# A hybrid attention and convolution layer: another order for deferred VectorE work, gate units and the first merge steps

## The reference

```
h    = rms_norm(x)
proj = h @ w_in                       # q k v z_a | glu (2048) | z_c | gate_a gate_c
A:  q, k rotated in part; 8 heads, two softmax maps of 64 dims each, causal
    o = softmax(q1 k1) v - lam * softmax(q2 k2) v
    y_attn = (rms_norm(o) * silu(z_a)) @ w_o_attn
B:  u = glu(...); causal depthwise conv of 31; layer_norm; silu
    y_conv = (u * silu(z_c)) @ w_pw2 + b_pw2
m   = sigmoid(gate_a) * y_attn + sigmoid(gate_c) * y_conv
out = x + rms_norm(m @ w_out)
```

## Time and profile before

| | us |
|---|---|
| median of 3 runs (1183.11 to 1189.87) | 1183.71 |
| the profiled execution | 1181.25 |
| its span on the slowest core, core 6 | 1179.7 |
| spans of the even cores 0, 2, 4, 6 | 1177.5, 1176.5, 1179.7, 1179.7 |
| spans of the odd cores 1, 3, 5, 7 | 1169.8, 1171.2, 1171.2, 1168.9 |
| PE busy on core 6 | 1096.0 (93%) |
| DVE busy | 551.1 (47%) |
| ACT busy | 323.7 (27%) |

### The profile page before, as it was taken

How to read it: one execution, slowest core, us unless ns; L and a number is a source line. 1 busy time by engine, 2 the same in 40 slices (tenths; PEclk the granted TensorE clock), 3 DMA queues, 4 the chain that set the end, 5 groups by cost and what they waited for, 6 DMA issues and landing times.

```text
span 1179.7 us, 21808 instructions; the slowest of 8 cores (1168.9 to 1179.7 us)
## 1 busy us (share of the span) xinstructions
PE 1096.0 (93%) x8042; PEld 674.0 (57%) x8042; DVE 551.1 (47%) x1290; ACT 323.7 (27%) x500; POOL 102.1 (9%) x196
## 2 busy tenths in 40 slices
PE   2699999999999998899888999999999999999995
PEld 1355556886666774577444566666666666654442
DVE  5573444426556136766677633333333333315333
ACT  3442223432101165566444311111111111102111
POOL 1111010011101100000000001101101010000000
PEclk9899999999999998899899999999999999999998
DMA  8929767554665632322142305337266183064442
GB/s 251 220 46 174 143 114 150 106 86 81 139 135 113 139 57 57 57 49 51 37 73 37 55 18 108 55 53 114 46 128 110 34 144 57 16 179 161 158 160 95
DMA packets 49792, 118.11 MB, mean 100 GB/s; under 512 B 5520, under 2 KB 11920, under 8 KB 46352
## 3 DMA queue, kind: packets, MB, share of 16 engines
q0 software_dynamic: 27648, 62.93, 32.8%
q1 hardware_dynamic: 21744, 53.53, 14.9%
q10 hardware_dynamic: 288, 0.18, 0.0%
HBM read 162.94 MB, written 16.58 MB: 152 GB/s over the span
## 4 chain that ended last, share of the span: by engine, by line
PE 81%; DVE 9%; issue 3%; DMA 3%; ACT 3%; DVEq 0%; SPq 0%; ACTq 0%
PE ps L1291 21%; PE ps L816 11%; PE ps L1343 11%; PE ps L770 10%; PE ps L649 9%; PE ps L1301 5%; PE ps L1295 5%; PE ps L693 3%; PE ps L1021 2%; PE ps L922 2%; DMA r<-usc 2%; PE ps L899 2%; DVE zoz L970 1%; DVE r L1028 1%; DVE r L958 1%
## 5 line engine op out<-in xcount | busy, mean ns | idle before, releaser
L1291 PE MATMUL ps<-hTo,wring 128*128 128x384 bf16 x1536 | 257.5, 326 | 0.0
L1291 PEld LDWEIGHTS ps<-hTo,wring 128*128 128x128 bf16 x1536 | 150.3, 98 | 99.2
L164 POOL DMA_DIRECT2D wring<-wp x176 | 93.4, 549 | 835.9 <-PE ps L1291 242.0
L649 PE MATMUL ps<-hTo,wring 128*128 128x384 bf16 x768 | 130.9, 332 | 9.9 <-ACT hTo L545 4.2
L770 PE MATMUL ps<-wring,hTo 128*128 128x256 bf16 x1152 | 135.6, 273 | 1.2 <-PE ps L899 1.2
L1308 ACT ACTIVATE zoz<-zoz 128x384 f32<-128x384 f32 x96 | 50.0, 522 | 315.3 <-DVE zoz L1306 315.3
L816 PE MATMUL ps<-hTo,wring 128*128 128x384 bf16 x768 | 125.0, 326 | 0.0
L770 PEld LDWEIGHTS ps<-wring,hTo 128*128 128x128 bf16 x1152 | 108.6, 98 | 21.2 <-issue 8.3
L1306 DVE TENSOR_TENSOR zoz<-ps,R 128x384 f32<-128x384 f32 x96 | 53.5, 558 | 128.0 <-PE ps L1291 127.8
L649 PEld LDWEIGHTS ps<-hTo,wring 128*128 128x128 bf16 x768 | 75.6, 100 | 63.1 <-issue 16.5
L905 ACT ACTIVATE r<-ps 128x1024 bf16<-128x1024 f32 (+2 forms) x104 | 92.8, 905 | 47.6 <-PE ps L899 44.2
(11 more groups left out here) (114 smaller groups left out, 1016.1 us busy)
## 6 DMA issues: line engine op xcount, KB each, us to landing
wring<-wp POOLq DMA_DIRECT2D x176, 256.0 KB, 7.1
r<-usc SPq DMA_DIRECT2D x32, 295.2 KB, 8.2
hTo<-xr SPq DMA_DIRECT2D x9, 1024.0 KB, 6.8
out<-hTo SPq DMA_DIRECT2D x18, 512.0 KB, 3.3
r<-xf SPq DMA_DIRECT2D x11, 768.0 KB, 9.2
r<-wop POOLq DMA_DIRECT2D x4, 1024.0 KB, 13.8
zoz<-wop POOLq DMA_DIRECT2D x4, 1024.0 KB, 14.9
r<-wout POOLq DMA_DIRECT2D x4, 1024.0 KB, 20.5
```

The source lines that it names most:

```text
L164: eng.dma_start(out=it[1][0], in_=it[1][1]).then_inc(self.dsem[it[2]], 16)
L649: t.op('pe', lambda e, dc=dc, x=x: e.matmul(bank(2 * par + x, n), lhsT=w[:, dc, 128 * x:128 * x + 128], rhs=hTo[:, dc, c:c + n], start=(dc ...
L1291: t.op('pe', lambda e, dc=dc, k=k, w=w, o=o, cs=cs, c0=c0, n=n: e.matmul(o[k], lhsT=w[:, dc, cs], rhs=hTo[:, dc, HALO + c0:HALO + c0 + n], ...
```

## The change

- **Deferred operations.** `spent` keeps an estimate of the time that TensorE and VectorE have been given so far; QK, masks, PV, fill pieces, z operations and deferred operations each add a constant. `pump` issues a deferred operation only if its `ready` time has come and VectorE's estimate is at most 0.5 us ahead of TensorE's. It is called at each step and after each fill piece. `H.rate` is gone.
- **z units.** With the last piece only the read from PSUM is issued. Tanh and the two products go to a list `zlate`, of which each step issues one entry: tanh one step later, the products a step after that. A new unit issues what is left first.
- **Quarters.** Half 0 has column blocks 0, 1 | 2, 3 | 4 | 5, 6, 7 of z, half 1 has 0 | 1 | 2, 3 | 4 to 7. Two weight panels change places accordingly.
- **Merge.** The step is split into `merge_head` (gates, conv branch) and `merge_tail` (the rest). Two heads, of steps 0 and 1, are issued before `f_begin`, which transposes with banks 2 and 6 instead of 6, 7, 4 and 5.

```diff
+++ after.py
@@ -208,15 +208,15 @@
     p = [rng(C_GLU + 128 * c, 128) + rng(C_GLU + 1024 + 128 * c, 128) for c in range(8)]
     p += [rng(C_ZA + 256 * g) for g in range(4)]
     p += [dims(C_Q, j) for j in range(4)] + [dims(C_K, j) for j in range(4)]
-    p += [rng(C_V), rng(C_V + 256), rng(C_ZC), rng(C_V + 512), rng(C_V + 768), rng(C_ZC + 256), rng(C_ZC + 512), rng(C_ZC + 768)]
+    p += [rng(C_V), rng(C_V + 256), rng(C_ZC), rng(C_V + 512), rng(C_ZC + 256), rng(C_V + 768), rng(C_ZC + 512), rng(C_ZC + 768)]
     for k in range(8):
         p += [rng(C_GA + 256 * k), rng(C_GC + 256 * k)]
     return p
 
 
 P_GLU, P_ZA, P_Q0, P_Q, P_K0, P_K, P_F = 0, 8, 12, 13, 16, 17, 28
-P_V = (20, 21, 23, 24)
-P_ZC = (22, 25, 26, 27)
+P_V = (20, 21, 23, 25)
+P_ZC = (22, 24, 26, 27)
 LAST = {0: 2, 1: 2, 2: 3}
 ND = 144
 
@@ -232,14 +232,14 @@
             self.xtg = ()
             self.fg = ((0, 384), (384, 384), (768, 384))
             self.slots = ((0, 2), (2, 2), (4, 2), (6, 2), (8, 1))
-            self.rate = 6
+            self.fill = ((('v', 1), ('z', 0, 1)), (('v', 2), ('z', 2, 3)), (('v', 3), ('z', 4)), (('z', 5, 6, 7),))
         else:
             self.first, self.no, self.halo, self.nx = 1152, 896, 32, 1152
             self.xg = ((0, 288), (288, 320), (608, 320))
             self.xtg = tuple((160 * k, 160) for k in range(7))
             self.fg = ((0, 448), (448, 448))
             self.slots = ((0, 1), (1, 2), (3, 2), (5, 2))
-            self.rate = 4
+            self.fill = ((('v', 1), ('z', 0)), (('z', 1), ('v', 2)), (('z', 2, 3), ('v', 3)), (('z', 4, 5, 6, 7),))
         self.nh = self.no + self.halo
         self.nu = self.no + 32
         self.nt = self.no // 128
@@ -886,6 +886,11 @@
 
 
     pairs = [(h,) + st for h in range(8) for st in H.steps()]
+    now = {'pe': 0.0, 'dve': 0.0}
+
+    def spent(e, us):
+
+        now[e] = (max(now['dve'], now['pe']) if e == 'dve' else now['pe']) + us
     NS = len(H.slots)
 
     def emit_qk(n):
@@ -901,6 +906,7 @@
                     rhs=QT[hp][64 * c:64 * c + 64, 128 * q0 + qo:128 * q0 + qo + qn], start=True, stop=True),
                     reads=rd, writes=[('ps', pb + c)], sig=(k == len(ent) - 1 and c == 1))
         w = sum(x[2] for x in ent)
+        spent('pe', w / 1280.0)
         src = ps[:, 512 * pb:512 * pb + 1024].rearrange("p (c n) -> p c n", c=2)[:, :, 0:w]
         t.op('act', lambda e: e.activation(out=et[:, :, 0:w], in_=src, func=AF.Exp, scale=0.125),
              reads=[('ps', pb), ('ps', pb + 1)], writes=[('ET', n % 3)])
@@ -909,6 +915,7 @@
                 v = et[:, :, o:o + 128]
                 t.op('dve', lambda e, v=v: e.tensor_tensor(out=v, in0=v, in1=tri.unsqueeze(1).to_broadcast([128, 2, 128]), op=ALU.mult),
                      reads=['cb', ('ET', n % 3)], writes=[('ET', n % 3)])
+                spent('dve', 0.3)
 
     def emit_pv(n):
         h, si, q0, nq, ent, first, last = pairs[n]
@@ -924,15 +931,31 @@
                     start=(begin and c == 0), stop=(final and c == 1)),
                     reads=[('ET', n % 3), ('VA', slot, kt), ('Vone', slot)], writes=[('ps', 4 + sub)],
                     sig=c == 1 and (i == len(todo) - 1 or final))
+        spent('pe', 0.16 * len(todo))
         if last:
             finalize(h, si, q0, nq)
 
     late = []
+    zlate = []
     oz_done = set()
 
     def run_late(n):
         for _ in range(min(n, len(late))):
-            late.pop(0)[1]()
+            _, _, cost, f = late.pop(0)
+            spent('dve', cost)
+            f()
+
+    def pump():
+
+        while late and late[0][1] <= now['pe'] and now['dve'] <= now['pe'] + 0.5:
+            run_late(1)
+
+    def run_zlate(flush=False):
+
+        while zlate:
+            zlate.pop(0)()
+            if not flush:
+                return
 
     def finalize(h, si, q0, nq):
         fk = NS * h + si
@@ -946,6 +969,7 @@
             t.op('act', lambda e: e.activation(out=ac, in_=src, func=AF.Copy), reads=[('ps', 4 + b) for b in range(nq)], writes=[an])
         else:
             t.op('dve', lambda e: e.tensor_copy(out=ac, in_=src), reads=[('ps', 4 + b) for b in range(nq)], writes=[an])
+            spent('dve', 0.7)
         f = [lambda: t.op('dve', lambda e: e.reciprocal(out=rs, in_=ac[:, :, :, 128]), reads=[an, 'small'], writes=[('rs', fk)]),
              lambda: t.op('dve', lambda e: e.tensor_scalar(out=rs[:, :, 1], in0=rs[:, :, 1], scalar1=neglam, scalar2=None, op0=ALU.mult),
                           reads=[('rs', fk), 'neglam'], writes=[('rs', fk)]),
@@ -961,7 +985,8 @@
                   lambda sub=sub, oi=oi, on=on, i=i: t.op('dve', lambda e: e.scalar_tensor_tensor(
                       out=t0s[:, sub, :], in0=oi, scalar=1.0, in1=oi, op0=ALU.mult, op1=ALU.mult, accum_out=ssqh[:, h, i:i + 1]),
                       reads=[on, 'small'], writes=['t0s', ('ssqh', h, i)])]
-        late.extend((fk, x) for x in f)
+        ready = now['pe'] + (2.0 if half == 0 else 0.0)
+        late.extend((fk, ready, 0.4, x) for x in f)
         if si == NS - 1:
             f = rsqrt_ops(rstdh[:, h, 0:NT], ssqh[:, h, 0:NT], NT, 1.0 / 128, 1e-5, [('ssqh', h, i) for i in range(NT)], [('rstdh', h)])
 
@@ -973,7 +998,7 @@
                 if i == NT - 1:
                     oz_done.add(h)
             f += [lambda i=i: scaled(i) for i in range(NT)]
-            late.extend((fk + 1, x) for x in f)
+            late.extend((fk + 1, ready, 0.3, x) for x in f)
 
     def att_stream():
         emit_qk(0)
@@ -981,7 +1006,8 @@
         for n in range(len(pairs)):
             if n + 2 < len(pairs):
                 emit_qk(n + 2)
-            run_late(H.rate)
+            run_zlate()
+            pump()
             yield 1.0
             emit_pv(n)
             if pairs[n][6]:
@@ -1025,12 +1051,20 @@
                 p = g % 2
                 uv = uT[:, cc, 32 + c0:32 + c0 + n]
                 zv, sv = zt[p][:, 0:n], zs[:, 0:n]
+                run_zlate(True)
                 t.op('dve', lambda e: e.tensor_tensor(out=zv, in0=bank(b, n), in1=rv, op=ALU.mult), reads=[('ps', b)] + rn, writes=[('zt', p)])
-                t.op('act', lambda e: e.activation(out=sv, in_=zv, func=AF.Tanh, scale=0.5), reads=[('zt', p)], writes=['zs'])
-                t.op('dve', lambda e: e.scalar_tensor_tensor(out=zv, in0=sv, scalar=1.0, in1=zv, op0=ALU.add, op1=ALU.mult),
-                     reads=[('zt', p), 'zs'], writes=[('zt', p)])
-                t.op('dve', lambda e: e.tensor_tensor(out=uv, in0=uv, in1=zv, op=ALU.mult),
-                     reads=[('zt', p), ('u2T', cc, g)], writes=[('u2T', cc, g)])
+                spent('dve', 0.6)
+
+                def tanh():
+                    t.op('act', lambda e: e.activation(out=sv, in_=zv, func=AF.Tanh, scale=0.5), reads=[('zt', p)], writes=['zs'])
+
+                def prods():
+                    t.op('dve', lambda e: e.scalar_tensor_tensor(out=zv, in0=sv, scalar=1.0, in1=zv, op0=ALU.add, op1=ALU.mult),
+                         reads=[('zt', p), 'zs'], writes=[('zt', p)])
+                    t.op('dve', lambda e: e.tensor_tensor(out=uv, in0=uv, in1=zv, op=ALU.mult),
+                         reads=[('zt', p), ('u2T', cc, g)], writes=[('u2T', cc, g)])
+                    spent('dve', 1.2)
+                zlate.extend((tanh, prods))
         return [lambda c=c: pc(c) for c in range(4)]
 
 
@@ -1212,24 +1246,21 @@
     per = len(pairs) // 4
     for g in range(4):
         fill = []
-        zcu = [(cc, k) for cc in ((0,), (1,), (2,), (3, 4, 5, 6, 7))[g] for k in range(NG)]
-        if g == 1:
-            for cc, k in zcu:
-                fill += zc_pieces(cc, k, fb)
-        if g < 3:
-            for u in units(0, NK):
-                fill += v_unit(g + 1, u, fb)
-        else:
+        if g == 3:
             t.handover(oth_res + lnbuf + ['cw', ('lj', 0), ('lj', 1)], ozT_all + [('wop', 0)] + ([('wop', 1)] if NX else []))
-        if g != 1:
-            turns = [f for h in range(6) for f in oz_turns(h, fb)]
-            for n, (cc, k) in enumerate(zcu):
-                fill += zc_pieces(cc, k, fb)
-                if g == 3 and n >= 2:
-                    left = len(zcu) - n
-                    for _ in range(-(-len(turns) // left)):
-                        fill.append(turns.pop(0))
-            assert g < 3 or not turns
+        turns = [f for h in range(6) for f in oz_turns(h, fb)]
+        for what in H.fill[g]:
+            if what[0] == 'v':
+                for u in units(0, NK):
+                    fill += v_unit(what[1], u, fb)
+            else:
+                zcu = [(cc, k) for cc in what[1:] for k in range(NG)]
+                for n, (cc, k) in enumerate(zcu):
+                    fill += zc_pieces(cc, k, fb)
+                    if g == 3 and n >= 2:
+                        for _ in range(-(-len(turns) // (len(zcu) - n))):
+                            fill.append(turns.pop(0))
+        assert g < 3 or not turns
```

(38 more changed lines are left out.)

49 lines of the change are left out of this document (18 added, 31 removed).

## The result

The changed kernel takes 1214.21 us (median of 4 runs, 1213.75 to 1215.17) against 1183.56: 1.025 of before, 95% interval 1.022 to 1.0281. It is slower by 30.7 us where 18.6 less were forecast.

A forecast was written before the change was run, and what follows sets the result against it. Bound: slowest core, stalled by instruction order. Even 1179.7 - 18.4 - 1.5 = 1160, odd 1171.2 - 11 + 0.5 = 1161; larger plus 1.55 is 1162.5, plus 2.46 profiled-to-median, 1165 us. Range 1157 to 1171 (60%).

The forecast's parts named there:

- The two kinds of core: Whole chip: slowest core sets the time, so even and odd predicted apart; even 1179.7 to 1160 us, odd 1171.2 to 1161.
- Work per quarter: Even cores' attention: larger engine's work per head gives quarters 59, 59, 51, 53 us, sum 222; 229 taken against 247.4 measured.
- The forecast of 1160 for the even cores: Even cores' end: 1179.7 less 18.4 us in the attention and 1.5 at the merge.
- the paragraph on pacing: Deferred operations: at most two of 0.4 us stand before a z bank's read; TensorE 28.5, VectorE 27.9 us per quarter-1 head.
- a backlog of 3 us: Half 0, quarter 3: 23.7 us of TensorE against 25.2 of VectorE per head; the four-slot accumulator rule lets the backlog through.
- The slower rival: Attention: z units bring quarter 4's stall to all quarters, 12 to 19 us more, 1192 to 1203 us; chance 9%.
- The end of the attention: Turn to merge: a second head of 6.5 us covers 3.1 us idle; net -1.5 us on half 0, +0.5 on half 1.
- The 1.6 us for two banks instead of four: Last transposes before the merge: head 7 waits about 1.6 us for the two copies of head 6.
- Tanh one step later: z units: VectorE's 0.78 us waits for tanh vanish, 18.8 us on core 6; counted as 1.7 against 2.5 per unit.
- The clock: Attention: idle TensorE lowers the clock, 17.3 us on core 6; spread waits could be worse than gathered ones.
- 6% of excess over work: Even cores' attention: work sum 234 against 247.4 us measured; the same 6% puts the bound at 236, against 222.

The follow-up runs named there:

- experiment 11: Kernel before, with only tanh one step later and products a step after; cores 4 and 6: 1176.8 and 1182.5 us, cores 5 and 7: 1154.3 and 1160.7.
- experiments 3: Kernel before, with only the pacing added (threshold 0.5 us); 1231.45 us in the profiled execution, even cores 1227.4 to 1229.9, odd 1161.5 to 1166.2.
- experiment 7: Kernel of experiment 5, with tanh and products right behind the z unit as before; even cores 1175.5 to 1178.1 us, odd 1158.7 to 1163.3.
- experiment 5: Changed kernel with VectorE's allowed lead 4 us on even cores, 0.5 us on odd; 1161.54 us, 0.9815 of before.
- experiment 8: Changed kernel with eight accumulator buffers instead of four on even cores, instruction order untouched; 1194.55 us.
- experiment 4: Changed kernel with the merge of before (one head ahead, four transpose banks); even cores 1221.5, 1218.8, 1217.3 and 1209.5 us, odd 1155.8 to 1163.0.

## Why the prediction was wrong

**The two kinds of core** were rightly kept apart, and the odd ones came out at 1156.9 to 1162.2 for 1161. The reason given was half right. The largest wait on core 7 was L948, 6.1 us, and is 1.9 now. But experiment 11 shows that tanh one step later alone brings it to 1.8 and the core to 1160.7, with the bursts of 4 left in. Pacing alone, in experiments 3 and 7, leaves it at 5.5 and 5.0 and brings the core to 1161.9 and 1163.3. So each of the two gives most of the gain by itself, and they overlap; the prediction took both as needed.

**Work per quarter** held in its sum. The sum of the larger engine per head was 222 us, with 229 taken for the attention of the even cores. With a threshold that works it is 218.9. The parts are less close, and that they cancel is luck: 53.6, 55.7 and 47.2 against 59, 59 and 51, but 62.4 against 53 in the fourth quarter. The forecast of 1160 for the even cores was nearer to experiment 5 (1150.5 to 1154.3, 6 to 10 us less) than to the kernel at hand.

**The step that failed** is the paragraph on pacing. It counted 28.5 us of TensorE and 27.9 of VectorE per head in the kernel's own constants, found "a backlog of 3 us" in quarter 3 which the accumulator rule (four slots) "lets through". Three things were wrong with it.

First, 0.6 us of margin per head is none. Over all eight heads the same constants charge each engine 223.2 us: there is no margin at all. Each head puts 22 operations (6.6 us) on the list at its end, beside a slot of 7 every few steps, and these are hardly worked off. The list holds 23 at the end of head 1 and 48 a slot later, 23 again at the end of head 2, 40 at that of head 3, and never less than 43 from head 4, the fifth, on. I compared sums per head where the length of the queue had to be followed slot by slot. Second, the estimate charges VectorE more than it takes. A z unit is charged 1.8 us and takes 1.7, a final operation 0.3 against (3.3 + 2.45) / 22 = 0.26; by the prediction's own durations (8 heads of 21.1 and 24 units of 1.7) it is 210 us of work for 223.2 charged. TensorE's 223.2 is near the 218.9 that the attention takes in experiment 5, its z pieces charged too high (0.8 for 0.65) and its V pieces too low (0.8 for 0.87). So the real VectorE was idle while the list was full: of its 72.6 us of waits at masks 32.7 lie behind 532 us, from the fifth head on. A pacing rule that may not catch up when the engine is idle has to be right on the mean. Third, the rule does not let a backlog through; it issues it, up to 29 operations at a time, right ahead of the copy that needs the buffer. In half 0 this copy stands on ScalarE among the exponentials. I named the masks, the bank reads and L948 as what is queued behind a deferred operation, and forgot that a buffer is waited for as well as a queue: 75 us of ScalarE, 36.1 of TensorE, 20 us of time (experiment 8).

**The slower rival** (9%, 1192 to 1203) had the right sign and the wrong mechanism. It wanted the estimate to run ahead of the chip so that `pump` bursts. It held back instead, and the burst came from the rule. Its price was too low also: the third quarter went from 52.3 to 69.2.

**The end of the attention.** The sum had -1.5 us, and said that a backlog there "is what the cover has to hold". At the last slot the rule issues 29 operations, and 48 more follow; VectorE is done with them 25 us after the attention's last PV (684.1 to 709.3, the end of the scalings in the timeline). The cover holds 13; 11 us were lost. The sentence was right and had no number. The 1.6 us for two banks instead of four had the right size: in experiment 5 TensorE waits 0.63 us between the transposes and 1.27 ahead of L1335, 1.1 more than the 0.84 ahead of L1301 in before.

**Tanh one step later** was costed as 0.78 us of VectorE per unit, 18.8 in all, folded into the work by engine. In experiment 7 it is worth 24 to 28. The missing part is ScalarE's: 51.7 us in which it stands at a tanh with exponentials behind it, and TensorE's wait for exponentials of 11.7 us instead of 1.0. The prediction named this order in the queue and gave it no price; the earlier trace rows showed one such wait of 7.14 us, and I read it as the burst's alone, where ScalarE's waits view of before has 54.9 us of it in 24 waits (410 to 720 us).

**The clock** followed the waits: 0.85 and 0.86 where TensorE is idle a quarter to a third of the time, 1.00 where it is busy 95%. Whether spread waits are worse than gathered ones was not tested: in experiment 5 the z units are spread and the clock is higher than before in all quarters (1.00, 1.00, 1.00 and 0.97 against 0.98, 0.90, 0.98 and 0.89), but its waits are mostly gone.

**Reading of size.** One half of the prediction's range was set by 6% of excess over work, taken from a kernel whose rate of 6 kept the list short (21 at most at a slot's end on the even cores, none issued by the rule). It could not bound what a new rule does to the list.

## What to carry to other kernels

When deferred work is paced by an estimate, follow the length of its list through the whole program before anything is run; a rule that holds it near its limit turns each forced issue into a burst just ahead of what needs the freed buffer. Leave margin (here 4 us of lead instead of 0.5, or the charges at 0.6) and set it for each program by what is queued on the paced engine: an accumulator copy on VectorE wants a short lead (4 us cost 7 to 14 here), one on ScalarE bears a longer one (4 us were good, 8 cost 7 to 9). And of two engines' in-order queues, ask which instruction waits at the head of which, since an activation that waits for VectorE holds up every exponential behind it.

## What the runs showed of the hardware that was not expected

Nothing of the chip itself was new. Two sizes are worth keeping: on these even cores a stop of ScalarE of 7 us becomes a stop of TensorE of 6.3 us, two steps of lead notwithstanding, and is followed by matmuls at the lower clock level, 1.2 GHz (0.24 us each against 0.13 ahead of the stop), in a quarter whose mean clock is 0.85. How much clock such stops cost is not fixed: in experiment 4 two cores with the same program and the same stretch were granted 0.85 and 0.90, and ended 8 us apart. And the pair of cores that share a sequence did not influence each other: the odd ones took 1154 to 1165 us over all executions both where the even ones ended at about 1152 (experiment 5) and where they ended at about 1212 (after).
